# A two-layer decoder step on one core: separate semaphores for the tiles of x, weights ahead of the mixer's output in quarters, and the last normalisation in a row

## What is computed

```python
xp = layer_norm(ALPHA * xp + hp, ln_g[i, 0], ln_b[i, 0])
fp, sp = conv_ffn(xp, zeros_prev, w_up[i], conv_w[i], conv_b[i], w_down[i])
xp = layer_norm(ALPHA * xp + fp, ln_g[i, 1], ln_b[i, 1])
...
def layer_norm(x, g, b):
    mu = xf.mean(-1, keepdims=True)
    var = jnp.square(xf - mu).mean(-1, keepdims=True)
    return (xf - mu) * lax.rsqrt(var + LN_EPS) * g + b
```

## Time and profile before

| | us |
|---|---|
| median of three runs | 3338.26 |
| the three runs | 3338.26, 3339.81, 3333.50 |
| the profiled execution, its own time | 3339.48 |
| its span, first to last instruction | 3337.7 |
| PE busy in it | 3150.4 |

### The profile page before, as it was taken

One profiled execution on the slowest core, in us unless ns is written; L12 is line 12 of the kernel. 1 busy time (PEld: TensorE's weight loads), 2 busy tenths in 40 slices (PEclk: granted clock), 3 DMA queues, 4 the chain that ended last, 5 costly groups with the idle time before them and its releaser, 6 DMA issues. The chain is left out here.

```text
span 3337.7 us, 56590 instructions
## 1 busy us (share of the span) xinstructions
PE 3150.4 (94%) x21560; PEld 3050.0 (91%) x21560; DVE 1775.4 (53%) x3631; ACT 1619.7 (49%) x3394; POOL 1695.4 (51%) x1416
## 2 busy tenths in 40 slices
PE   7999999999999967999999999589879999999997
PEld 7999999999999947999999999588878999999996
DVE  3445455454554537765464465348857653533543
ACT  3554555555555514454353354247744543543543
POOL 4554555555555504665465465243336664554662
PEclk9999999999999978999999999799989999999998
DMA  5665666666667275344444444211153434444442
GB/s 180 237 238 200 246 242 213 228 239 240 223 220 263 82 286 186 124 133 128 138 135 137 142 139 144 87 47 39 46 168 114 139 124 141 154 136 138 163 144 95
DMA packets 134669, 540.73 MB, mean 162 GB/s; under 512 B 24816, under 2 KB 49184, under 8 KB 131568
## 3 DMA queue, kind: packets, MB, share of 16 engines
q1 hardware_dynamic: 133200, 535.79, 47.9%
q10 hardware_dynamic: 784, 1.12, 0.1%
q0 software_dynamic: 416, 0.21, 0.0%
HBM read 497.34 MB, written 216.90 MB: 214 GB/s over the span
## 5 line engine op out<-in xcount | busy, mean ns | idle before, releaser
L1228 ACT CAST t_w_hi<-t_raw 128x1024 fp32r<-128x1024 f32 (+1 forms) x456 | 468.4, 1027 | 759.3 <-PE t_bank L103 758.3
L101 PE MATMUL t_bank<-x_hi,t_w_hi 128*128 128x352 f32 (+1 forms) x2112 | 680.9, 322 | 5.6 <-DVE x_lo L1513 2.8
L1347 POOL TENSOR_TENSOR t_w_lo<-t_raw,t_w_hi 128x1024 fp32r<-128x1024 f32 (+1 forms) x228 | 546.3, 2396 | 258.9 <-ACT t_w_hi L1228 258.9
L102 PE MATMUL t_bank<-x_lo,t_w_hi 128*128 128x352 f32 (+1 forms) x2112 | 675.2, 320 | 0.0
L103 PE MATMUL t_bank<-x_hi,t_w_lo 128*128 128x352 f32 (+1 forms) x2112 | 672.0, 318 | 0.0
L1420 DVE TENSOR_TENSOR t_w_lo<-t_raw,t_w_hi 128x1024 fp32r<-128x1024 f32 (+1 forms) x228 | 320.7, 1406 | 656.2 <-ACT t_w_hi L1228 656.2
L101 PE MATMUL a_gemm<-x_hi,a_w_hi 128*128 128x352 f32 (+1 forms) x1728 | 564.4, 327 | 19.2 <-DVE x_lo L621 19.2
L102 PE MATMUL a_gemm<-x_lo,a_w_hi 128*128 128x352 f32 (+1 forms) x1728 | 554.6, 321 | 0.0
L103 PE MATMUL a_gemm<-x_hi,a_w_lo 128*128 128x352 f32 (+1 forms) x1728 | 552.4, 320 | 0.0
L101 PE MATMUL t_bank<-t_h_hi,t_w_hi 128*128 128x352 f32 (+1 forms) x1440 | 467.7, 325 | 39.3 <-DVE t_h_lo L1426 31.2
L103 PE MATMUL t_bank<-t_h_hi,t_w_lo 128*128 128x352 f32 (+1 forms) x1440 | 464.9, 323 | 0.0
(11 more groups left out here) (275 smaller groups left out, 5908.1 us busy)
## 6 DMA issues: line engine op xcount, KB each, us to landing
t_raw<-w_up SPq DMA_DIRECT2D x264, 512.0 KB, 3.7
roll<-cache SPq DMA_DIRECT2D x128, 1023.5 KB
t_raw<-w_down SPq DMA_DIRECT2D x96, 512.0 KB, 3.6
a_raw<-w_a SPq DMA_DIRECT2D x72, 512.0 KB, 4.4
roll<-cache SPq DMA_DIRECT2D x16, 2044.0 KB
t_raw<-w_o SPq DMA_DIRECT2D x48, 512.0 KB, 3.6
t_raw<-w_down SPq DMA_DIRECT2D x48, 384.0 KB, 3.2
vT<-a_vt SPq DMA_DIRECT2D x24, 516.0 KB, 7.2
```

Source lines behind the costliest of these rows:

```text
L101: pe.matmul(out, w_hi, x_hi, start=first, stop=False)
L102: pe.matmul(out, w_hi, x_lo, start=False, stop=False)
L1228: act.copy(w_hi[:, b % RING, cols], raw[:, b % RING, cols]).then_inc(s_whi, 1)
L1347: pool.tensor_tensor(w_lo[:, b % RING, cols], raw[:, b % RING, cols], f32(w_hi[:, b % RING, cols]), ALU.subtract).then_inc(s_wlo[0], 1)
```

## The change

It changes five things. (1) Mixer A: each tile of x has a semaphore, SP waits for none of them, block 1 is issued right after the first six, and tiles 6 and 7 ahead of the constants; POOL waits for the constants one body step sooner. (2) Trunks: block 0 is loaded and cast first; the mixer's output comes in four quarters of two feature tiles, for every chunk; in block 0 PE waits for each quarter where it needs it. (3) The last stage of the trunk follows a list of its own, `LAST`, for both layers: four centrings, four squares, three additions; its squares 2 and 3 have buffers of their own (parts of `acc` and `zt`). (4) In the last stage of layer 1, gain and offset of the odd tiles move to POOL, with a semaphore `s_yodd`. (5) Mixer B: DVE's low part of block 0 stands ahead of its wait for the constants. What isn't shown are declarations and the same renaming of halves to quarters.

```diff
@@ -334,16 +335,14 @@
 
             load_block(0)
             for i in range(6):
-                sp_e.dma_start(o[:, i // NG, i % NG, :], dram["xT"][i * P:(i + 1) * P, :]).then_inc(s_xin, 16)
-                sp_e.wait_ge(s_xin, 16 * (i + 1)) if i == 5 else None
+                sp_e.dma_start(o[:, i // NG, i % NG, :], dram["xT"][i * P:(i + 1) * P, :]).then_inc(x_in[i], 16)
             load_block(1)
+            for i in range(6, KT):
+                sp_e.wait_ge(s_xlo, i - 5)
+                sp_e.dma_start(o[:, 0, i - 6, :], dram["xT"][i * P:(i + 1) * P, :]).then_inc(x_in[i], 16)
             for dst, name in ((cos, "cos"), (sin, "sin"), (mask, "mask_a"), (mask3, "mask_c"), (ident, "ident")):
                 sp_e.dma_start(dst[:, :], dram[name]).then_inc(s_const, 16)
             sp_e.dma_start(vt[0:16, 0:QT * P], dram["sel"]).then_inc(s_const, 16)
-            for i in range(6, KT):
-                sp_e.wait_ge(s_xlo, i - 5)
-                sp_e.dma_start(o[:, 0, i - 6, :], dram["xT"][i * P:(i + 1) * P, :]).then_inc(s_xin, 16)
-                sp_e.wait_ge(s_xin, 16 * (i + 1))
             load_block(2)
...
@@ -428,7 +427,7 @@
 
             split_w(0)
             for i in range(KT):
-                act.wait_ge(s_xin, 96 if i < 6 else 16 * (i + 1))
+                act.wait_ge(x_in[i], 16)
                 act.copy(x_hi[:, i, :], o[:, (i % 6) // NG, i % NG, :]).then_inc(s_xhi, 1)
...
@@ -584,7 +583,7 @@
             def body(u, i, s):
                 if s in SPLIT_AT and 3 * (i + 1) + SPLIT_AT[s] < NB:
                     split_w(3 * (i + 1) + SPLIT_AT[s])
-                if i == -1 and s == 1:
+                if i == -1 and s == 0:
                     pool.wait_ge(s_const, 16 * 6)
                 if projects(i):
...
@@ -1039,6 +1038,8 @@
 NORM += [("fold", 0, 5), ("var", 0, 6), ("dev", 0, 6), ("inverse", 0, 6)]
 NORM += [x for k in range(4) for x in (("scale", k, 7 + k), ("high", k, 7 + k), ("affine", k, 8 + k), ("low", k, 9 + k))]
 NORM.sort(key=lambda x: x[2])
+LAST = [("mean", 0)] + [(x, k) for x in ("center", "square") for k in range(4)] + [("add", k) for k in (1, 2, 3)]
+LAST += [("fold", 0), ("var", 0), ("dev", 0), ("inverse", 0)] + [(x, k) for x in ("scale", "high", "affine", "low") for k in range(4)]
...
-        def o_part(c, half):
+        def o_part(c, q):
 
 
             n = CHUNKS[c][1]
-            stage = (h_hi, h_lo)[half]
-            a = 8 * (c % 2) + 4 * half
-            return f32(stage[:, 16:20, 0:n]), h_hi[:, a:a + 4, 0:n], h_lo[:, a:a + 4, 0:n]
+            stage = (h_hi, h_lo)[q // 2][:, 16 + 2 * (q % 2):18 + 2 * (q % 2), 0:n]
+            a = 8 * (c % 2) + 2 * q
+            return f32(stage), h_hi[:, a:a + 2, 0:n], h_lo[:, a:a + 2, 0:n]
+
+        def squared(stage, k, n):
+
+
+            buf = (acc, zt)[k - 2] if stage == N_STAGES - 1 and k > 1 else sq
+            return buf[:, 0:2, 0:n]
...
-            def load_o(c, half):
+            def load_o(c, q):
                 off, n = CHUNKS[c]
-                need(sp, s_olo, 2 * (c - 1) + half + 1)
-                sp.dma_start(o_part(c, half)[0],
-                             dram["o_scr"].rearrange("(m p) t -> p m t", p=P)[:, 4 * half:4 * half + 4, off:off + n]
-                             ).then_inc(o_in[half], 16)
+                need(sp, s_olo, 4 * (c - 1) + q + 1)
+                sp.dma_start(o_part(c, q)[0],
+                             dram["o_scr"].rearrange("(m p) t -> p m t", p=P)[:, 2 * q:2 * q + 2, off:off + n]
+                             ).then_inc(o_in[q], 16)
...
-            load_o(0, 0)
             load_w(0)
-            load_o(0, 1)
+            for q in range(4):
+                load_o(0, q)
...
                 if kind == "o" and m == 5 and c + 1 < NCH:
-                    load_o(c + 1, 0)
-                    load_o(c + 1, 1)
+                    for q in range(4):
+                        load_o(c + 1, q)
...
                 for k in range(KT // 2):
-                    need(sp, s_y, KT * (N_STAGES - 1) + 2 * k + 2)
+                    need(sp, s_y, KT * (N_STAGES - 1) + k + 1)
+                    need(sp, s_yodd, k + 1)
...
-                    need(act, s_red, 4 * stage + k - 1)
-                    act.activation(sq[:, :, 0:n], two(zz, k, n), ACT.Square).then_inc(s_sq, 1)
+                    if stage == N_STAGES - 1 and k == 2:
+                        act.wait_ge(s_hlo, NCH * FT)
+                    need(act, s_red, 4 * stage + (0 if stage == N_STAGES - 1 else k - 1))
+                    act.activation(squared(stage, k, n), two(zz, k, n), ACT.Square).then_inc(s_sq, 1)
...
                 for m in (2 * k, 2 * k + 1):
+                    if stored(stage) and stage == N_STAGES - 1 and m % 2:
+                        continue
                     if stored(stage):
                         act.activation(z[:, stage % 2, m, 0:n], z[:, stage % 2, m, 0:n], ACT.Identity,
                                        scale=ln[:, part, 0, m:m + 1], bias=ln[:, part, 1, m:m + 1]).then_inc(s_y, 1)
@@ -1301,9 +1313,9 @@
...
-            split_o(0, 0)
             split(0)
-            split_o(0, 1)
+            for q in range(4):
+                split_o(0, q)
             split(1)
...
@@ -1313,8 +1325,8 @@
                 if tile_before(b):
                     evacuate_z(b, *tile_before(b))
                 if kind == "o" and m == 6 and c + 1 < NCH:
-                    split_o(c + 1, 0)
-                    split_o(c + 1, 1)
+                    for q in range(4):
+                        split_o(c + 1, q)
...
-            for what, k, at in NORM:
+            for what, k in LAST:
                 norm(N_STAGES - 1, what, k)
...
+                if what == "affine" and stored(stage) and stage == N_STAGES - 1:
+                    m = 2 * k + 1
+                    pool.wait_ge(s_norm, 4 * stage + k + 1)
+                    pool.tensor_scalar(z[:, zp, m, 0:n], z[:, zp, m, 0:n], ln[:, part, 0, m:m + 1],
+                                       ln[:, part, 1, m:m + 1], ALU.mult, ALU.add).then_inc(s_yodd, 1)
...
-            split_o(0, 0)
-            split_o(0, 1)
+            for q in range(4):
+                split_o(0, q)
             split(1)
...
-                    if m in (0, 4):
-                        pe.wait_ge(s_olo, 2 * c + 2)
+                    if m == 0 and c > 0:
+                        pe.wait_ge(s_olo, 4 * c + 4)
...
                 for kt in range(nk):
+                    if b == 0 and kt % 2 == 0:
+                        pe.wait_ge(s_olo, kt // 2 + 1)
...
+            split(0)
             dve.wait_ge(s_const, 16 * 6)
             dve.tensor_scalar(nsink[:, :], nsink[:, :], -1.0, None, ALU.mult)
             dve.tensor_scalar(bias[:, 3:], bias[:, 3:], -SCALE, None, ALU.mult).then_inc(s_prep, 1)
-            split(0)
             for b in range(3):
```

More of the change, by code:

```diff
@@ L222, in mixer_a @@
         x_bank = ps("vT_factors")
-        s_const, s_xin, s_xhi, s_xlo, s_sel = (sem(x) for x in ("const", "xin", "xhi", "xlo", "selr"))
+        s_const, s_xhi, s_xlo, s_sel = (sem(x) for x in ("const", "xhi", "xlo", "selr"))
+        x_in = [sem(f"x_in{i}") for i in range(KT)]
         w_in = [sem("w_in0"), sem("w_in1")]
@@ L1103, in trunk @@
         s_const, s_bias, s_ohi, s_olo, s_set = (sem(x) for x in ("const", "bias", "ohi", "olo", "set"))
-        o_in = [sem("o_in0"), sem("o_in1")]
+        o_in = [sem(f"o_in{i}") for i in range(4)]
         w_in = [sem(f"w_in{i}") for i in range(RING)]
@@ L1490, in add_squares @@
                 need(dve, s_red, 4 * stage + k - 1)
-                dve.tensor_tensor(sums2[:, :, 0:n], sums2[:, :, 0:n], sq[:, :, 0:n], ALU.add).then_inc(s_red, 1)
+                dve.tensor_tensor(sums2[:, :, 0:n], sums2[:, :, 0:n], squared(stage, k, n), ALU.add).then_inc(s_red, 1)
             def fold_squares(stage):
```

16 lines of the change are left out of this document (8 added, 8 removed).

## The result

The changed kernel took 3312.65 us, the median of six runs (3307.73 to 3323.47), against 3335.05 us for the kernel before in the same session (six runs): a ratio of 0.9936, 95% interval 0.9923 to 0.9948. The prediction was 3315.0 in a range of 3309 to 3324. The profiled execution took 3310.81 us, 3309.0 of it span. The page's part 1, beside the earlier trace rows: PE's busy time fell by 9 us only, so 20 of the 28.7 us between the two spans are time in which PE stood still.

What follows compares the result with a forecast made beforehand. TensorE, busy 94% of the span, bounds the kernel, so only its standstills count: 8.4+3.0+2.4+3.8+3.1+2.6 = 23.3 us off 3338.26 us, the median, gives 3315.0 us, range 3309 to 3324.

Steps and rivals of the forecast that it cites:

- mixer A, eighth tile: Mixer A's start: tiles land every 1.27 us, PE takes the eighth at 18.2 instead of 26.64; 8.4 us, bounds 7.4 to 10.
- head of trunk 0: Trunk 0's start: weights first and quarters bring PE's first matmul 8.1 us after the first issue instead of 11.09; 3.0 us.
- last normalisation, trunk 0: End of trunk 0: centrings, squares and additions in a row bring the fold sooner; 2.4 us, bounds 1.4 to 3.4.
- head of mixer B: Mixer B's start: first weights' low part no longer waits for the constants, starting at 2160.42 instead of 2164.23; 3.8 us.
- head of trunk 1: Trunk 1's start: weights first and quarters bring PE's first matmul 8.1 us after the first issue instead of 11.18; 3.1 us.
- last normalisation, trunk 1: End of the run: row order and odd tiles on POOL end it at 33.6 instead of 36.25; 2.6 us, nearly all squares.
- Rival 1: Mixer A: a time-bound stream sets its end, so the 8.4 us are lost; 14.9 us gained, 3323.4; chance 6%.
- Rival 3: Mixer A: x6 waits for a buffer and the queue runs dry; 5.4 in place of 8.4 us, 3318; chance 5%.
- rival 2: Trunk heads: quarters land in series, 2.4 us each, taking 1.5 from each trunk; 20.3 gained, 3318; chance 4%.
- the lower bound, "POOL held off until the scales end": Last normalisation of trunk 1: POOL's steps wait until the scales end at 29.15, last store at 34.9; gain only 1.4 us.
- Each restart may gain or lose up to 1.2, together about 2: TensorE's clock at the four restarts: noise, since a us at 1.2 GHz instead of 2.4 loses half of it.
- Rival 4: Long stretches: granted clock falls because PE idles less; 0.7% uses up 23 us, 1.0% makes it 8 us slower; chance 2%.

Runs made afterwards that it cites:

- e10: The changed kernel with mixer A's second weights loaded behind the last two x tiles instead of ahead of them; 3321.40 us in one run.
- e1: The kernel before with only a semaphore for each x tile and the last two tiles' loads ahead of the constants; 3321.54 us, ratio 0.9954.
- e5: The changed kernel with the mixer's output in halves again, the weights still first; 3317.30 us, ratio 0.9946.
- e7: The changed kernel with VectorE instead of GpSimd making the first weights' low part in both trunks; 3312.18 us, ratio 0.9936.
- e4: The kernel before with only mixer B's first low part moved ahead of the wait for the constants; 3330.92 us, ratio 0.9980.
- e6: The changed kernel with all eight affine steps of the very last normalisation on ScalarE again; 3312.97 us in one run.
- e12: The changed kernel with unread TensorE products ahead of the first blocks, 36 in each trunk and 24 in mixer B; 3309.94 us, ratio 0.9914.

## Why the prediction came out right, step by step

| place | predicted gain | in the trace |
|---|---|---|
| mixer A, eighth tile | 8.4 | 26.64-18.34 = 8.30 |
| head of trunk 0 | 3.0 | 11.09-7.92 = 3.17 |
| last normalisation, trunk 0 | 2.4 | 24.58-22.02 = 2.56 |
| head of mixer B | 3.8 | 9.79-5.94 = 3.85 |
| head of trunk 1 | 3.1 | 11.18-7.95 = 3.23 |
| last normalisation, trunk 1 | 2.6 | 22.19-20.82 = 1.37 |
| sum | 23.3 | 22.5 |

- **Mixer A.** The chain of the prediction stands tile by tile: casts from 5.74 at 1.27 us, the eighth tile at 18.34 (18.2). The step that the queue alone sets this was tested by e10. Rival 1 (the shift is lost inside) falls with e1, whose mixer A is 11.6 us shorter than the shortest without this part; over all traces the means are 10.5 apart, though e5, with this part, has 1246.9. Rival 3 (the queue runs dry) falls with the casts: the seventh comes two slots behind the sixth, one of them the weights'.
- **Trunk heads.** 7.92 and 7.95 against 8.1. VectorE behind GpSimd's subtraction was the last step, as written; e7 shows it by taking it away. Quarters that land in series (rival 2) are refuted by the casts of the first two, 1.0 us apart, and the next two back to back. The figures of the Trainium skill that the prediction sets against the quarters ("DMA: Bandwidth & Descriptors", Anatomy of one DMA, and Bandwidth) are given there for DMAs that GpSimd issues; here SP issues them, and none of the gaps came near the 2.8 us of the estimate.
- **Mixer B.** 3.85 for 3.8. VectorE's small steps on the constants came at 2147.73 and PE waited for none of them. What I hadn't weighed are PE's waits further on, which take back some 1.4 us on average (e4 above).
- **Last normalisations.** The row order gave its 2.33 us in both (8.09 and 8.08 to 5.76). In trunk 0 a little more came, within its bounds. In trunk 1 the term was mis-sized by 1.2 us, and the step that failed is the choice of value for GpSimd beside VectorE: I took 1.30 us for a step, from the earlier trace rows, where the two take turns; the lower bound, "POOL held off until the scales end", is what happened, 1.37 against 1.4. The pitch of the stores wasn't kept either: they ran together in the queue. In e6 the whole 1.0 us is GpSimd's half: the part that was meant to unload ScalarE costs time, and the squares alone bring 2.35.
- **Clock.** "Each restart may gain or lose up to 1.2, together about 2" was the right cause and too small. Between the profiled pair the low level took 9.2 us less, and two traces of one program differ by 6.2 us in mixer A, about half of it by the clock. I had counted the four restarts and not the pauses inside the stages, at which the clock sometimes falls. The medians hid this; the profiled pair alone would have put the gain at 28.7. That the medians' 22.4 us lie within 1 us of the 23.3 is partly luck: the interval goes from 17 to 26 us, and the repeat of the same kernel gave 27.8. Rival 4 (a falling clock eats the gain) has a small true core at most: e12's lead in the trunks was gone behind the next pauses. In the long stretches the clock didn't fall; over the span it is 0.974 where it was 0.970.

## What to carry to other kernels

Sum a change over the places where the bottleneck engine stands still, place by place, and hold the sum against the median of runs and not against one pair of traces: here the places repeated within some 0.6 us, with one exception of 1.0, and the stretches between them only within 11. One trace of each kernel isn't enough to tell whether such a stretch pays a gain back; averages over many traces were needed to see that mixer B returns 1.4 of its 3.8 us as waits. Before work is moved to an idle engine at a kernel's end, look whether the two engines can run beside each other and whether the results leave earlier; a half that comes late and in a bunch is worse than none. Work of no use that keeps TensorE's clock up through one pause may only move the fall to the next.

## What the runs showed of the hardware

- A GpSimd step of 0.61 us took 2.48 us beside VectorE's scalings in a row (changed kernel); GpSimd's subtraction (2.34 us) held a VectorE quarter of 0.84 us back for 1.2 (e7).
- TensorE's clock behind a pause of 2.4 us fell to 0.50 in one execution and stayed at 1.00 in another of the same program (the changed kernel, mixer A); at the pause 49 us into a trunk it fell in 7 of 24, and in 4 of 4 with PE kept busy through the trunk's head.
- Behind PE's start in a trunk the clock stayed at 0.50 for 3.1 to 6.1 us, whether PE started 8 or 11 us into it.
- The load queue landed a tile of 516 KB every 1.27 us (by the casts of x); the stores at the end ran at 363 GB/s when four stood in the queue.
